# One 8 KB gather per expert row into a ring of eight places, in a streaming encoder step on one core

## What is computed

```
h = x + jnp.einsum('btm,md->btd', mix, w_o)
y = h + peer(rmsnorm(h, norm2))

def block(xb):                                   # 128 tokens
    q = einsum('nd,dk->nk', xb, wq).reshape(128, 8, 2, 64)
    s = einsum('nhcd,hckd->nhck', q, subkeys)
    sv, si = top_k(s, 16)                        # per head and half
    cand = sv[:, :, 0, :, None] + sv[:, :, 1, None, :]
    fv, fi = top_k(cand, 16)                     # 16 of 256 pairs
    eidx = ...                                   # 16 experts of 16384, per head
    g = softmax(fv)
    act = gelu(einsum('nd,nhkd->nhk', xb, u[eidx]))
    return einsum('nhk,nhkd->nd', g * act, v[eidx])
```

## Time and profile before

| | |
|---|---|
| median of 3 runs | 1261.18 us (1260.83 to 1262.43) |
| span of the profiled execution, first to last instruction | 1192.3 us |
| median less span | 68.9 us |
| TensorE, mean granted clock | 0.984 of full |
| PE busy / DVE / ACT / POOL | 88% / 67% / 30% / 62% of the span |
| moved by DMA | 468.12 MB, mean 393 GB/s |
| of these by gathers | 402.70 MB |

### The profile page before, as it was taken

How to read it: one execution, slowest core, us unless ns; L and a number is a source line. 1 busy time by engine, 2 the same in 40 slices (tenths; PEclk the granted TensorE clock), 3 DMA queues, 4 the chain that set the end, 5 groups by cost and what they waited for, 6 DMA issues and landing times.

```text
span 1192.3 us, 11355 instructions
## 1 busy us (share of the span) xinstructions
PE 1048.0 (88%) x3311; PEld 511.3 (43%) x3311; DVE 793.0 (67%) x1943; ACT 362.9 (30%) x853; POOL 735.0 (62%) x774
## 2 busy tenths in 40 slices
PE   9999999999868987898979899997888888778886
PEld 4767565664325543433535355442223222223332
DVE  2639986998765588998546575784674664773344
ACT  2535235324131343333322333321212212222120
POOL 0004565566655677777746566776776777776774
PEclk9999999999989999999989999999999999999999
DMA  9967999999999999999999999999999999999997
GB/s 373 411 231 252 410 412 412 360 398 409 406 401 409 384 368 390 409 409 408 415 408 408 410 408 404 406 408 414 409 409 410 408 410 409 409 409 376 410 409 303
DMA packets 125628, 468.12 MB, mean 393 GB/s; under 512 B 14072, under 2 KB 17152, under 8 KB 123392
## 3 DMA queue, kind: packets, MB, share of 16 engines
q0 software_dynamic: 110592, 402.70, 85.4%
q1 hardware_dynamic: 14976, 64.70, 13.6%
HBM read 462.86 MB, written 4.42 MB: 392 GB/s over the span
## 4 chain that ended last, share of the span: by engine, by line
DMA 26%; PE 20%; POOL 14%; DVE 8%; issue 6%; ACT 0%; POOLq 0%; DVEq 0%; ACTq 0%
DMA UV<-in_p_v,EIDX 18%; PE PSUM L1978 14%; POOL UV L579 8%; DMA UV<-in_p_u,EIDX 7%; POOL UV L564 6%; DVE UV L1475 3%; PE PSUM L1757 2%; PE PSUM L1731 1%; PE PSUM L1700 1%; PE PSUM L1774 1%; POOL UV L572 1%; DVE SEL L213 0%; DVE SEL L219 0%; DVE UV L215 0%; DVE SEL L211 0%
## 5 line engine op out<-in xcount | busy, mean ns | idle before, releaser
L1978 PE MATMUL PSUM<-UV,DIAG 128*128 128x512 f32 x1500 | 727.2, 617 | 124.9 <-DMA UV<-in_p_v,EIDX 119.2
L1475 DVE CUSTOM_DVE_ANT_0 UV<-UV,PSUM 128x1024 f32<-128x1024 f32 x384 | 462.9, 1218 | 269.7 <-DMA UV<-in_p_u,EIDX 265.8
L564 POOL DMA_INDIRECT UV<-in_p_u,EIDX x384 | 367.2, 956 | 254.5 <-issue 97.1
L1978 PEld LDWEIGHTS PSUM<-UV,DIAG 128*128 128x128 f32 x1500 | 267.3, 192 | 523.4 <-DMA UV<-in_p_v,EIDX 293.6
L579 POOL DMA_INDIRECT UV<-in_p_v,EIDX x376 | 358.6, 954 | 186.4 <-PE PSUM L1978 104.4
L1001 ACT ACTIVATE DIAG<-CST,WGT 128x128 f32<-128x128 f32 x375 | 149.1, 401 | 697.0 <-PE PSUM L1978 696.3
L1558 PE MATMUL PSUM<-WR,XW 128*128 128x512 f32 (+1 forms) x128 | 50.6, 554 | 0.1
L1567 PE MATMUL PSUM<-XW,WR 128*128 128x256 f32 x192 | 42.3, 379 | 0.0
L1567 PEld LDWEIGHTS PSUM<-XW,WR 128*128 128x128 f32 x192 | 36.5, 190 | 6.8 <-issue 1.9
L1558 PEld LDWEIGHTS PSUM<-WR,XW 128*128 128x128 f32 x128 | 24.2, 190 | 25.3 <-issue 22.7
L211 DVE MAX8 SEL<-UV 128x8 f32<-128x128 f32 (+1 forms) x71 | 21.5, 330 | 15.6 <-ACT UV L604 12.6
(11 more groups left out here) (292 smaller groups left out, 818.7 us busy)
## 6 DMA issues: line engine op xcount, KB each, us to landing
WR<-in_w_o SPq DMA_DIRECT2D x13, 512.0 KB, 8.2
UV<-in_p_u,EIDX POOLq DMA_INDIRECT x384, 10.5
UV<-in_p_v,EIDX POOLq DMA_INDIRECT x384, 10.5
WR<-in_p_wq SPq DMA_DIRECT2D x10, 512.0 KB, 7.4
UV<-in_w_o SPq DMA_DIRECT2D x2, 2048.0 KB, 14.6
UV<-in_p_wq SPq DMA_DIRECT2D x2, 2048.0 KB, 9.7
WR<-in_w_B SPq DMA_DIRECT2D x2, 2048.0 KB, 8.1
UV<-in_w_B SPq DMA_DIRECT2D x4, 512.0 KB, 6.5
```

Of the source, the lines that this page charges most:

```text
L564: nc.gpsimd.indirect_dma_start(UBUF[n % RU], None, a["p_u"], bass.IndirectOffsetOnAxis(EIDX[:, n:n + 1], 0)).then_inc(u_got[n % RU], 16)
L1475: v.tensor_tensor_reduce(out=row, in0=row, in1=XNP, scale=1.0, scalar=0.0, op0=ALU.mult, op1=ALU.add, accum_out=DOTS[:, i % 2, s:s + 1]).t ...
L1978: ins = mm(bank[6 + k][:, :], DIAG[:, m % ND, :], VBUF[m % RV][:, k * 512:(k + 1) * 512], start=False, stop=m % SLOTS == SLOTS - 1 or m == ...
```

## The change

- **One gather.** The host lays `p_u` and `p_v` side by side as `p_uv`, 8 KB a row. One gather (L560 of the changed kernel) brings 128 of these, 1 MB, into one of eight places `ROWS`; 384 gathers stand where 768 stood. The eighth place is a new tile `EIGHTH` of 8 KB a partition; the descriptors' scratch is halved to 8 KB for it.
- **One ring.** A place is free when its v half has been used, by TensorE (`row_summed`) or VectorE (`row_added`). `LAGS`, and with it the lead of u over v, is gone: the slot is the row for both.
- **Weights row by row.** ScalarE takes the GELU of one row's dots (L950), multiplies with a gate that VectorE has already divided by its sum (L953, `gate_ready`), and writes `DIAG` (L961). VectorE's step of L1466 is gone.
- **VectorE adds 16 rows of tile 0** (5, 11, ... 95) to h; TensorE adds h behind row 127. At the end VectorE adds rows 382 and 383 only; before, it added rows 369, 371, ... 381, 382 and 383.
- **Tile 1's front in quarters.** Each unit is four parts at slots +0, +1, +3, +4; the order of the front's steps and the slots of all trunks are new, and none of it stands ahead of the first sum.

```diff
-RU, RV, ND = 8, 6, 6
-LAGS = ((0, 28), (50, 50), (200, 45), (300, 30), (320, 30), (371, 13), (384, 13))
-UNIT_SLOT = [2, 5, 8, 12, 16, 20, 24, 27, 31, 34, 42, 45, 49, 57]
+RING, ND, NW = 8, 6, 32
+UNIT_SLOT = [1, 7, 13, 19, 25, 30, 35, 42, 50, 56, 64, 70, 78, 84]
+ADDED = [*range(5, 96, 6), 382, 383]
+SUMMED = [n for n in range(HEADS * PK) if n not in ADDED]
...
-            def gather_u(n):
+            def gather(n):
                 if n % PK == 0:
                     pool.wait_ge(heads_chosen, n // PK + 1 + (n > 0))
                 elif n == 8:
                     pool.wait_ge(heads_chosen, 2)
-                if n >= RU:
-                    pool.wait_ge(u_free, n - RU + 1)
+                if n == 4:
+                    take(pool, ("qq", 0, 3))
+                elif n == 6:
+                    take(pool, ("qq", 0, 7))
+                elif n >= RING and n - RING in ADDED:
+                    pool.wait_ge(row_added, done_before(n - RING, ADDED) + 1)
+                elif n >= RING:
+                    pool.wait_ge(row_summed, done_before(n - RING, SUMMED) + 1)
                 nc.gpsimd.indirect_dma_start(
...
+                    ROWS[place_of(n)], None, a["p_uv"], bass.IndirectOffsetOnAxis(EIDX[:, n:n + 1], 0)
+                ).then_inc(row_got[place_of(n)], 16)
...
+            def weigh(n):
+                i, at = n // PK, slice(n % NW, n % NW + 1)
+                act.wait_ge(dot_done, n + 1)
+                own.done(nc.scalar.activation(GELU[:, at], DOTS[:, at], ACT.Gelu))
+                if n % PK == 0:
+                    act.wait_ge(gate_ready, i + 1)
+                weight = nc.scalar.activation(WGT[:, at], GELU[:, at], ACT.Copy, scale=GATE[:, n:n + 1])
...
+                if n < SLOTS and n - 1 in ADDED:
+                    add(n - 1, X[0], X[0], row_added)
                 fronts(n)
...
             def unit(n):
                 chunk, k = UNITS[n]
...
+                for part, slot in enumerate((0, 1, 3, 4)):
+                    yield UNIT_SLOT[n] + slot
+                    w = later_weights(chunk)
+                    if chunk[0] == "B" or chunk == "AI":
+                        rows_of(name, XNT12[:, k - 1], w, 2 * part, 2 * part + 2)
+                    else:
+                        two_heads(name, w, k, part)
...
-            trunks(slot_at(0) - 1)
+            trunks(-1)
...
-    o["p_u"], o["p_v"] = i["p_u"][0], i["p_v"][0]
+    o["p_uv"] = np.concatenate([i["p_u"][0], i["p_v"][0]], axis=1)
...
+    nc = bacc.Bacc("TRN2", target_bir_lowering=False, num_devices=1, dynamic_dma_scratch_size=8192)
```

More of the change, by code:

```diff
@@ L161, in in_slots, with place_of, done_before @@
     return upto
-def slot_at(n):
-    for (a, la), (b, lb) in zip(LAGS, LAGS[1:]):
-        if n < b:
-            return n + la + (lb - la) * (n - a) // (b - a)
-    return n + LAGS[-1][1]
-def v_row(m):
-    return m if m < ALONE else ALONE + 1 + 2 * (m - ALONE)
-SUMS = ALONE + 6
-BORROWED = {ALONE + 2 * k: TURN + k for k in range(RU)}
+ADDED = [*range(5, 96, 6), 382, 383]
+SUMMED = [n for n in range(HEADS * PK) if n not in ADDED]
+def place_of(n):
+    return n % RING
+def done_before(n, rows):
+    return sum(r < n for r in rows)
 def choice_slot(t, h):
@@ L963, in _ @@
             square_h(0)
[L965 to L973 removed]
+            first, trunks, gated = in_slots(choices(0)), in_slots(trunk()), in_slots(gates())
             first(CHOICES[0] + 6)
@@ L1017, in _ @@
-            for m in range(SUMS):
-                weigh(m)
+            fronts(-1)
+            for n in range(HEADS * PK):
+                weigh(n)
+                if n and n % SLOTS == 0:
+                    read_y(n // SLOTS - 1)
+                fronts(n)
             fronts(ALL)
@@ L1511, in _ @@
+            dve.wait_ge(wgt_done, len(ADDED))
+            for k in range(2):
+                cols = slice(k * 512, (k + 1) * 512)
+                v.scalar_tensor_tensor(out=X[2][:, cols], in0=VROW[place_of(383)][:, cols], scalar=WGT[:, 383 % NW:383 % NW + 1],
+                                       in1=X[2][:, cols], op0=ALU.mult, op1=ALU.add).then_inc(y_last, 1)
         @block.tensor
@@ L1546, in later_weights, with rows_of @@
                 return view(WR, s * WCOLS, KC, W_IN[chunk][1])
-            def rows_of(name, x, w):
+            def rows_of(name, x, w, c0=0, c1=KC):
                 n = w.shape[2]
-                pb = start(name)
-                for c in range(KC):
+                pb = start(name) if c0 == 0 else bank[PLACE[name][0]]
+                for c in range(c0, c1):
                     if name == ("bp", 0, 0) and c and c % 2 == 0:
```

477 lines of the change are left out of this document (198 added, 279 removed).

## The result

The changed kernel takes 1252.36 us (median of 4 runs, 1247.13 to 1254.58). The kernel before took 1261.81 us (4 runs, 1260.83 to 1262.73). The ratio is 0.9908, 95% interval 0.9883 to 0.9933: faster by 0.9%, where 2.6% was forecast. That is inside the range and has the sign that was forecast, but it is 24 us from the forecast time.

| chip | kernel before, us | changed kernel, us | ratio, 95% |
|---|---|---|---|
| first result | 1261.8 | 1252.4 | 0.9908 (0.9883 to 0.9933) |
| e runs | 1254.1 | not run | |
| f runs | 1263.1 | 1255.0 | 0.9898 (0.9836 to 0.996) |
| g runs | 1263.2 | not run | |
| h runs | 1195.6 | not run | |

A forecast was written before the change was run, and what follows sets the result against it. DMA transfers were taken as the bound, TensorE barely in rows 0 to 127: 112.4 + 376 = 488 us, + 620 + 36 + 8 = 1152, 7 more to a span of 1159, with 68.9 around it 1228 us; range 1203 to 1270.

The forecast's parts named there:

- The base: Around the loop: the 68.9 us by which the median exceeds the profiled span, added unchanged to the forecast span.
- The number of gathers: On POOL: 384 gathers of some 0.95 us instead of 768, off the path either way, so priced at nothing.
- A row's transfer: In the gathers: 2.46 us for an 8 KB row against 2.56 before, up to 38 us gained over 384 rows.
- rival B: In the gathers: the wide row moves no faster, a row stays at 2.56 us, 1253 us in all; chance 0.13.
- The start: Before the loop: first gather at 94.6 us, first dot at 109.3, sums from 112.4; 5 us of DMA idle.
- Stage 1: Rows 0 to 127: TensorE barely the bound, need about 360 us at 96% busy, 376 us, row 128 summed at 488.
- the point of decision: In rows 0 to 127: TensorE's busy share of 88%, from which the slower case of engines waiting in a ring decides.
- Rows 128 to 256: First part of rows 128 to 383: transfers bind at 2.46 us a row, plus 36 us of loads and 8 of loss.
- Behind row 256: Last part of rows 128 to 383: rows 2.46 us apart; over 2.5 us would show the forecast wrong.
- The 7 us of the end: After the last landing at 1152 us: a dot, GELU and weight, and the two halves, 7 us to the end.
- Rival C: Rows 0 to 127, on TensorE: engines wait for each other in a ring, 427 us, 1279 in all, slower; chance 0.18.
- the chance of 0.60: The chance given to the forecast's own case, a time of 1210 to 1248 us.

The follow-up runs named there:

- e1: The kernel before, unchanged, profiled anew on a slow chip: 1254.18 us, ratio 0.9998.
- h1: The kernel before with eight places for v rows instead of six and halved descriptor scratch, on a quick chip: 1195.74 us, ratio 1.0006.
- i1: The changed kernel, unchanged, run again on a quick chip: 1250.88 us, where the kernel before took 1195.6.
- i2: The changed kernel with two gathers of 4 KB rows into each place instead of one, on a quick chip: 1262.39 us, ratio 1.0555.
- f2: The changed kernel with the front's steps two rows later on ScalarE and VectorE up to slot 104, on a slow chip: 1233.28 us, ratio 0.9734.
- g3: The changed kernel with tile 1's and tile 2's front steps two rows later on ScalarE and VectorE, on a slow chip: 1210.69 us, ratio 0.959.
- h4: g3's kernel with GELU replaced by a copy, leaving out most table loads, on a quick chip: 1192.50 us, ratio 0.9976.
- e3: The changed kernel with GELU replaced by a copy, leaving out 77 of 107 table loads: 1226.67 us, ratio 0.9783.
- h2: g3's kernel with tile 1's front units whole again instead of in quarters, on a quick chip: 1217.87 us, ratio 1.0194.
- h3: g3's kernel with VectorE adding 23 rows of tile 0 instead of 16, on a quick chip: 1217.61 us, ratio 1.0196.

## Why the prediction was off

The forecast was 33 us faster, and 9 came. Against the forecast's span of 1159 us the changed kernel's is 1250.0, 91 us more, and 67 of them were hidden by an error of the other sign in what lies around the span (68.9 taken, 1.8 measured). That the time came within 24 us and the sign held was luck: against the trace that it was read from, the prediction had a span 33 us shorter, and the span is 58 us longer. In its order:

- **The base, wrong.** The prediction put the 68.9 us between the profiled span of 1192.3 and the median of 1261.18 around the span and left them there. They were inside the loop, between two kinds of chip (e1, h1, i1). A gap of 6% between a trace and the times is a sign that the trace is not of the executions that were timed, and it should have been a term with bounds.
- **The number of gathers "off the path either way", wrong on slow chips.** On them two gathers a row instead of one cost the changed kernel 7.2% (1.0623 / 0.9908), on quick ones 0.9% (i2 over i1).
- **A row's transfer, right.** 2.46 us forecast from the earlier trace rows, 2.49 measured; rival B fell. The 1.1% that the Trainium skill gives for it (DMA: Bandwidth & Descriptors, section Why small descriptors are slow) is less than the 2.9% between 409 GB/s in the earlier trace rows and 421 here. The preference of the same page of the Trainium skill for packets of at most 4096 B (section SWDGE vs HWDGE vs iDMA) is not borne out for the gathers, which ran faster in 8 KB packets; SP's loads beside them landed later (i1, i2), which the prediction had no term for.
- **The start, 7 us short.** First gather at 95.1 us and first dot at 109.8 us as forecast. The first sum is at 119.4 and not 112.4, since the gate of row 0 stands behind the copies of the last heads' scores on ScalarE, with a table load ahead of it and one behind. VectorE's and ScalarE's timelines:

```profile
116.38 0.16 DVE L1261 RECIPROCAL SEL<-SEL 128x1 f32<-128x1 f32 x1 [5.34 <-ACT GATE L755]
```

```profile
112.83 1.57 ACT L574 ACTIVATE UV<-PSUM,SMALL 128x128 f32<-128x128 f32 x4
114.43 0.20 ACT L754 ACTIVATE SMALL<-SEL 128x1 f32<-128x1 f32 x1
114.65 1.28 ACT L755 ACT_TABLE_LOAD   x1
...
117.03 1.28 ACT L950 ACT_TABLE_LOAD   x1
```

- **Stage 1, the step that failed: 376 us forecast, 433.5 measured, 57 us.** TensorE's need was 371 and not 360; its share 86%, under the 88% that was named as the point of decision, and not 96%. The 11 us of need can be the clock (an estimate): granted were 0.95 over 433.5 us, 21.7 us lost, where the earlier trace rows have 1.00 and 0.95 over 197.6 and 209.6 us, 10.5 us lost. The forecast took 96% on the ground that TensorE has the most to do and that the quarters leave no long gap. But the rows' weights now wait behind front steps on ScalarE, which wait for TensorE. f2 and g3 show it: with these steps two rows later 20 to 28 us return. Of what remains (405.9 - 364.4 = 42 us idle) h4 gives the table loads 8 or more, 13.5 are waits for SP's loads, and for the rest no run has a cause of its own.
- **Rows 128 to 256: 359 us forecast (315 of transfer, all 36 of loads, 8 of loss), 374.7 measured, 16 us.** SP moved 10.49 MB here, some 25 us, and 128 rows at 2.49 us are 319, so the loss was about 31 us and not 8, by estimate. It is the same wait (g3 takes 11 to 19 us off), with table loads (e3, h4).
- **Behind row 256: 312 us forecast, 322.4 measured, 10 us.** A row is 2.55 us instead of 2.46 on average (dots of rows 256 to 383, 920.6 to 1244.2 us), over the 2.5 us that was named as a sign of being wrong: 2.49 for its transfer, and 3.15 MB of SP's loads between the rows. The 7 us of the end hold. The row ahead of the last had landed when its dot started at 1241.02 us and rows are 2.49 us apart, so the last landed at about 1243.5, 6.5 us ahead of the end. Its dot, its two half additions and the stores:

```profile
1244.24 1.22 DVE L1426 CUSTOM_DVE_ANT_0 UV<-UV,PSUM 128x1024 f32<-128x1024 f32 x1
...
1246.06 1.42 DVE L1435 SCALAR_TENSOR_TENSOR XW<-UV,WGT,XW 128x512 f32<-128x512 f32 x2 [0.60 <-ACT WGT L953]
1246.84 0.99 SPq L453 DMA_DIRECT2D out_y<-XW  x2
```

The four misses are 7 + 57 + 16 + 10 = 90 of the 91 us. Rival C named the mechanism and the place. Its 427 us for stage 1 are 6 short of what came, and counted from the same kind of execution its verdict "slower" is what the quick chips show. What the chance of 0.60 rested on was a share read where the weights had 28 to 50 rows of lead.

The best version that ran is g3: the change with the front's steps two rows later on ScalarE and VectorE. At 0.959 it beats both kernels on a slow chip. On a quick one nothing that computes everything beat the kernel before: g3 was not run there, and its nearest kin, h2 and h3, are 1.9% above it.

## What to carry to other kernels

When a change takes away a lead of many rows between the making of a weight and its use, price the new chain at the worst stretch of the trace and not at the best. In-order engines that serve both the chain and other work wait for each other even where none is full; moving the other work's follow-up steps a little later, without touching the engine that they follow, gave back up to 42 us here (1252.4 to 1210.7, on two chips). Compare the profiled span with the timed median before anything else: here they lay 1.8 us apart in every execution that was both timed and profiled, and 68.9 us apart where they were of different executions, and the gain read from the one did not exist in the other.
